# Mixture of experts on Trainium2: a pair's down product ahead of the next pair's second up product

## The chip, the cores and the metric

The kernel runs on one core of one Trainium2 chip. A core has TensorE for matrix products, VectorE, ScalarE and GpSimd for everything elementwise, SyncE for issuing transfers, and 16 transfer engines that all queues share. The metric is the device time of one execution in microseconds. The median of several runs counts. Beside it one execution was profiled; its rows are quoted below.

## The reference

Two transformer-like blocks follow each other, over 512 tokens of width 1024, in float32. The change concerns the second half of the first block, a mixture of 32 experts of which each token takes two:

```python
e_w, e_idx = lax.top_k(jax.nn.softmax(e_logits, axis=-1), TOP_K)      # TOP_K = 2
weight = g_gate * e_w
...
hid = jax.nn.silu(jnp.einsum('td,edf->tef', tk, w1)) * jnp.einsum('td,edf->tef', tk, w3)
hid = hid * c[:, :, None].astype(hid.dtype)
return jnp.einsum('tef,efd->td', hid, w2)
```

w1 and w3 are 1024x256 for each expert and w2 is 256x1024: 1.048 MB each, 100.7 MB over all experts. The rest (a spatial gate and an attention with differences ahead of the experts; a delta rule and a stick-breaking attention behind them) is untouched by the change.

## The kernel before, in words

The program is written by hand: `tensor`, `vector`, `scalar`, `gpsimd` and `sync` each issue one engine's instructions, in the order in which they stand, and wait on each other by semaphores. An engine never passes a wait. What stands behind it in the program waits too.

**Pairs.** The experts are taken two at a time, 16 pairs (expert n and n + 16). Each expert has 64 places for tokens, so a pair fills the 128 partitions. For pair m:

- GpSimd's `gather` (the transfer at L2737) fetches the pair's token rows from `xn_scratch` in HBM by the table `slot_tokens` into one of two buffers `XG`. 1024 rows of 4 KB are fetched in all. It waits for `bring(m - 2)` to have read the buffer.
- TensorE's `bring` (L826; its transposes are at L526, eight of 128x128) turns the rows. ScalarE's and VectorE's `half_tokens` copy a half each to `TOK`.
- TensorE's `up(m, 0)` (L836, matmuls at L848) is the product with w1. ScalarE's `gate_half` takes its sigmoid and VectorE's `gated` multiplies (L1708).
- `up(m, 1)` is the product with w3. VectorE multiplies it in, with the token's weight, in the second part of `gated` (L1713).
- `hand_over` (L854, two transposes at L526, called the hidden turns below) turns the hidden layer and ScalarE's `hidden` copies it to `HT`.
- `down` (L863, matmuls at L876) is the product with w2, in two halves. ScalarE's and VectorE's `half_rows` (VectorE's is L1721) copy a half each to `YO`.
- GpSimd's `add_rows` (the scatter, L2748) adds the rows of `YO` to `x2_scratch` in HBM, one scatter at a time.

The transposes of `bring` are called the token turns below. Most of ScalarE's work has the line of a helper, L2134.

**TensorE's order before** is

```python
bring(0)
for m in range(PAIRS):
    up(m, 0)
    if m:
        hand_over(m - 1)
    else:
        bring(1)
    up(m, 1)
    if m:
        down(m - 1)
        if m + 1 < PAIRS:
            bring(m + 1)
```

and GpSimd's is gather 0, gather 1, then for each m: gather(m + 2), scatter(m). So gather(m + 2) stands behind scatter(m - 1).

**Weights.** SyncE's `load` (L2808) brings the 96 weight matrices of the experts as units of 1.048 MB, six for a pair, in the order of the list `units` that `pair_up` and `pair_down` fill. They land in 19 buffers in turn (`landing_order`: parts of `y_plain`, `raw`, `w_plain`, `h_plain`, `merged` and `scratch`), and TensorE reads them there. A load into a buffer waits until the product that read the unit before is done. `unit` tells a product where its units begin.

Behind the experts, SyncE reads `x2_scratch` back (L2869) when the last scatter has landed, and the second block begins with a norm.

Of the kernel before, what the change touches and what calls it, by code (L numbers as in the profile page):

```python
# [109 lines left out]
def build(nc, x, norm1_g, w_in, v_norm_g, w_s, b_s, q_norm_g, k_norm_g, lambda_q1, lambda_k1,  # L110
# [9 lines left out]
    KD = D // P  # L120
# [12 lines left out]
    PAIRS = NE // 2  # L133
# [154 lines left out]
    units, unit = [], {}  # L288
# [7 lines left out]
    def pair_of(m):  # L296
        return m, m + PAIRS

    def pair_up(m):
        unit["up", m] = len(units), 4  # L300
        for w in (w1, w3):
            for n in pair_of(m):
                units.append([(lambda a: a.rearrange("p (k f) -> p k f", k=KD),
                               w[0, n].rearrange("(p k) f -> p k f", k=KD))])

    def pair_down(m):
        unit["down", m] = len(units), 2
        for n in pair_of(m):
            units.append([(lambda a: a.rearrange("p (k n) -> p k n", k=2),
                           w2[0, n].rearrange("(p k) n -> p k n", k=2))])  # L310
# [22 lines left out]
    MOE = len(units)  # L333
    for m in range(PAIRS + 1):
        if m < PAIRS:
            pair_up(m)
        if m:
            pair_down(m - 1)
    TWO = len(units)
    for b in range(3):  # L340
        matrix(("qa", b), W_IN2, D, BANK * b)
# [68 lines left out]
    def inside(*key):  # L410

        return PS[:, bank.of[key] if not pe.counting else 0, :]
# [102 lines left out]
    def tensor(e):  # L515
# [132 lines left out]
        for b in range(2):  # L648
            product("va", b, False, hthi, htlo, by_k=lambda k: ve["out", "n1", k])
            if b == 0:  # L650
                on.wait_ge(*po["spatial"])
                for half in range(2):
                    ps = fresh("wst", half)
                    for g in range(4):
                        m = turn(ps[:, g * P:g * P + P], wsn[:, half * 4 + g, :])
# [9 lines left out]
            for g in range(4):  # L665
# [4 lines left out]
                for i in range(NT):  # L670
                    m = e.matmul(ps[:, i * P:i * P + P], vn_a[:, i, g * P:g * P + P], wst[:, gg, :], start=True,
                                 stop=True)
# [134 lines left out]
        for j in range(NT):  # L807
            m = e.matmul(rp[:, j + 1:, :], ones, both[:, j, :].unsqueeze(1).broadcast_to([P, NT - j, NE]), start=False,
                         stop=j == NT - 1, skip_group_check=True)
# [4 lines left out]
        for n in range(2 * NT):  # L814
            m = e.matmul(ps[:, 0:COLS], is_place[:, n, :], val[:, 0, n, :], start=n == 0, stop=n == 2 * NT - 1)
# [4 lines left out]
        for n in range(2 * NT):  # L820
            m = e.matmul(ps[:, 0:COLS], is_place[:, n, :], val[:, 1, n, :], start=n == 0, stop=n == 2 * NT - 1)
# [4 lines left out]
        def bring(m):  # L826

            on.wait_ge(*xg_got[m % 2][m])
            for a in range(2):
                ps = fresh("bring", m, a)  # L830
                for k in range(HB):
                    t = turn(ps[:, k * P:k * P + P], XG[:, m % 2, a * HB + k::KD])
                t.then_inc(*pe.mark("bring", m, a))
                bank.filled(("bring", m, a))

        def up(m, a):  # L836

            u, j = m % 2, unit["up", m][0] + 2 * a
            ps = fresh("up", m, a)
            w = [raw_place(j + x).rearrange("p (k f) -> p k f", k=KD) for x in range(2)]  # L840
            on.wait_ge(*ac["out", "bring", m, 0])
            on.wait_ge(*ve["out", "bring", m, 1])
            for x in range(2):
                on.wait_ge(*raw_got[raw_slot[j + x]][j + x])
            for k in range(KD):
                for x in range(2):
                    rows_ = slice(x * CAP, x * CAP + CAP)
                    t = e.matmul(ps[rows_, 0:DE], TOK[:, u, k, rows_], w[x][:, k, :], start=k == 0, stop=k == KD - 1)  # L848
            t.then_inc(*pe.mark("up", m, a))
            for x in range(2):  # L850
                pe.also("unit", j + x)
            bank.filled(("up", m, a))
# [30 lines left out]
        for m in range(PAIRS):  # L883
            up(m, 0)
            if m:
                hand_over(m - 1)
            else:
                bring(1)
            up(m, 1)
            if m:  # L890
                down(m - 1)
                if m + 1 < PAIRS:
                    bring(m + 1)
        hand_over(PAIRS - 1)
        down(PAIRS - 1)

# [3 lines left out]
        with e.If(v):  # L900
# [4 lines left out]
            for j in range(EXTRA):  # L905
                more.wait_ge(*ov_xg[j])
                for k in range(KD):
                    m = e.transpose(OVT[:, k // HB, k % HB * P:k % HB * P + P], oxg[:, k::KD], ident)
# [3 lines left out]
                for k in range(KD):  # L912
                    m = e.matmul(OVU, ogt[:, k, :], w13[:, :, k, :], start=k == 0, stop=k == KD - 1)
                m.then_inc(*ov_pe.mark("up", j))
                more.wait_ge(*ov_ve["gated", j])
                for k in range(2):
                    m = e.transpose(OVT[:, 0, k * P:k * P + P], osg[:, k::2], ident)
                m.then_inc(*ov_pe.mark("hidden", j))
                more.wait_ge(*ov_ve["hidden", j])
                for half in range(2):  # L920
                    cols = slice(half * BANK, half * BANK + BANK)
                    for k in range(2):
                        m = e.matmul(OVD[:, half, :], oht[:, k, :], wdn[:, k, cols], start=k == 0, stop=k == 1)
# [25 lines left out]
        for k in range(KD):  # L949
            m = passes(ps[0:NB, :], wbah[:, k, :], wbal[:, k, :], hthi[:, k, :], htlo[:, k, :], k == 0, k == KD - 1)  # L950
# [293 lines left out]
    def vector(e):  # L1244
# [453 lines left out]
        def half_tokens(m):  # L1698
            on.wait_ge(*pe["bring", m, 1])
            if m > 1:  # L1700
                on.wait_ge(*pe["up", m - 2, 1])
            e.tensor_copy(TOK[:, m % 2, HB:, :], inside("bring", m, 1).rearrange("p (k n) -> p k n", k=HB)).then_inc(
                *ve.mark("out", "bring", m, 1))

        def gated(m):
            u = m % 2
            on.wait_ge(*ac["sigmoid", m])
            tt(SG[:, u, :], SG[:, u, :], inside("up", m, 0)[:, 0:DE], MUL).then_inc(*ve.mark("out", "up", m, 0))  # L1708
            on.wait_ge(*pe["up", m, 1])
            if m > 1:  # L1710
                on.wait_ge(*pe["hidden", m - 2])
            settle()
            stt(HID[:, u, :], SG[:, u, :], info[:, m:m + 1], inside("up", m, 1)[:, 0:DE], MUL, MUL).then_inc(  # L1713
                *ve.mark("out", "up", m, 1))
            ve.also("hid", m)
# [5 lines left out]
            e.tensor_copy(YO[:, m % 2, BANK:], inside("down", m, 1)).then_inc(*ve.mark("out", "down", m, 1))  # L1721

        half_tokens(0)
        half_tokens(1)
        for m in range(PAIRS):
            gated(m)
            if m:
                half_rows(m - 1)
                if m + 1 < PAIRS:
                    half_tokens(m + 1)  # L1730
        half_rows(PAIRS - 1)
        split()
        ve.also("experts")
# [381 lines left out]
    def scalar(e):  # L2115
# [287 lines left out]
        def half_tokens(m):  # L2403
            on.wait_ge(*pe["bring", m, 0])
            if m > 1:
                on.wait_ge(*pe["up", m - 2, 1])
            act(TOK[:, m % 2, 0:HB, :], inside("bring", m, 0).rearrange("p (k n) -> p k n", k=HB), ACT.Copy).then_inc(
                *ac.mark("out", "bring", m, 0))
# [7 lines left out]
        def hidden(m):  # L2416
            on.wait_ge(*pe["hidden", m])
            if m > 1:
                on.wait_ge(*pe["down", m - 2, 1])
            act(HT[:, m % 2], inside("hidden", m)[:, 0:2 * P].rearrange("p (k n) -> p k n", k=2), ACT.Copy).then_inc(  # L2420
                *ac.mark("out", "hidden", m))
# [8 lines left out]
        for m in range(PAIRS):  # L2430
            gate_half(m)
            if m:
                hidden(m - 1)
            else:
                half_tokens(1)
            if m:
                half_rows(m - 1)
                if m + 1 < PAIRS:
                    half_tokens(m + 1)
        hidden(PAIRS - 1)  # L2440
        half_rows(PAIRS - 1)
        split()
# [494 lines left out]
```

## Time and profile before

| | |
|---|---|
| median of 3 runs | 1462.85 us (1461.64 to 1464.62) |
| the profiled execution, its own time | 1465.2 us |
| its span, first to last instruction | 1463.4 us |
| TensorE matmuls busy | 1327.1 us, 91% |
| TensorE granted clock, mean share | 0.962 |
| VectorE, ScalarE, GpSimd busy | 46%, 34%, 4% |
| HBM read | 196.33 MB |
| 16 transfer engines, weights' and other loads' queue | 34.6% |

Busy times are shares of the whole span, which has stages with different limits; the expert stage lies at about 600 to 850 us. The granted clock is a share of 2.4 GHz: 1.0 is that, 0.50 is 1.2 GHz, and values between are mixtures within the stretch. "DMA share" is the mean busy share of the 16 transfer engines (rounding takes it to 1.02 when they are full). In an instruction's row the names are those of the program's buffers, output first, and the bracket at its end has the idle time ahead of it and what ended that. float32 products and transposes appear in the profile twice as often as in the program.

### The profile page before, as it was taken

Reading aid. Unit: us, or ns where it says so; the run is one execution under the profiler, and the core shown is the slowest. Engines: PE = TensorE matmul, PEld = TensorE weight load, DVE = VectorE, ACT = ScalarE, POOL = GpSimd, SP = SyncE. Lnnn points to the kernel's source line nnn. Section 1 sums busy time; section 2 is a strip of 40 time slices with the busy share of each in tenths; the row PEclk is TensorE's granted clock in tenths of the full one; section 3 lists DMA queues with packets and bytes.
Section 4 is the critical chain, followed back from the end, with each engine's and each line's share of the span. In section 5 each row is a group of like instructions: output and inputs, shape, how many; then the busy total and the mean of one; then the engine's idle time right before and its main releaser. Section 6 shows DMA issues by size and latency. Waiting matters only on the chain.

```text
span 1463.4 us, 16683 instructions
## 1 busy us (share of the span) xinstructions
PE 1327.1 (91%) x7019; PEld 1019.3 (70%) x7019; DVE 677.3 (46%) x1045; ACT 494.9 (34%) x768; POOL 53.6 (4%) x59
## 2 busy tenths in 40 slices
PE   6999999999998996788887839999989989899998
PEld 5888887668766885555544428777968876578887
DVE  4454335765577446211111148747566454413253
ACT  4333234446345423011111144444232235422231
POOL 0000000000000000011211100000000000000000
PEclk9999999999999997699999969999999999899999
DMA  6222322112222368899999942102010020112331
GB/s 220 85 87 87 115 73 75 55 58 87 87 86 87 119 239 326 338 401 402 408 402 409 348 133 86 58 1 72 16 51 9 29 87 1 58 58 86 106 124 58
DMA packets 67268, 205.85 MB, mean 141 GB/s; under 512 B 9091, under 2 KB 10229, under 8 KB 54902
## 3 DMA queue, kind: packets, MB, share of 16 engines
q1 hardware_dynamic: 60658, 190.02, 34.6%
q0 software_dynamic: 5824, 12.60, 3.0%
q10 hardware_dynamic: 708, 2.13, 0.4%
q8 instruction: 57, 0.93, 0.3%
q14 instruction: 21, 0.17, 0.0%
HBM read 196.33 MB, written 16.78 MB: 146 GB/s over the span
## 4 chain that ended last, share of the span: by engine, by line
PE 71%; DVE 11%; DMA 10%; ACT 5%; issue 3%; POOL 0%; SPq 0%; DVEq 0%; POOLq 0%; ACTq 0%
PE PS L529 16%; PE PS L531 16%; PE PS L530 16%; PE PS L994 5%; PE PS L526 4%; DMA work<-xn_scratch,slot_tokens 4%; PE PS L848 3%; DMA raw<-in_w 2%; DMA scratch<-in_w 2%; PE PS L876 2%; PE PS L1172 2%; DVE wlo L1263 2%; DVE smalls L1255 1%; ACT work L2134 1%; PE PS L714 1%
## 5 line engine op out<-in xcount | busy, mean ns | idle before, releaser
L1263 DVE TENSOR_TENSOR wlo<-raw,whi 128x2048 fp32r<-128x2048 f32 x72 | 164.9, 2290 | 280.9 <-ACT whi L2134 280.7
L2134 ACT ACTIVATE whi<-raw 128x2048 fp32r<-128x2048 f32 x72 | 137.6, 1911 | 236.3 <-PE PS L531 219.9
L529 PE MATMUL PS<-whi,hthi 128*128 128x512 f32 x480 | 196.0, 408 | 5.7 <-ACT y_plain L2134 4.1
L529 PE MATMUL PS<-hthi,whi 128*128 128x512 f32 x480 | 197.9, 412 | 0.8 <-DVE htlo L1296 0.8
L2134 ACT ACTIVATE work<-PS 128x512 f32<-128x512 f32 (+3 forms) x150 | 82.6, 563 | 316.2 <-PE PS L876 91.3
L531 PE MATMUL PS<-hthi,wlo 128*128 128x512 f32 x480 | 188.7, 393 | 0.0
L530 PE MATMUL PS<-htlo,whi 128*128 128x512 f32 x480 | 188.4, 392 | 0.0
L531 PE MATMUL PS<-whi,htlo 128*128 128x512 f32 x480 | 188.2, 392 | 0.0
L530 PE MATMUL PS<-wlo,hthi 128*128 128x512 f32 x480 | 188.1, 392 | 0.0
L529 PEld LDWEIGHTS PS<-hthi,whi 128*128 128x128 f32 x480 | 91.0, 190 | 32.7 <-issue 14.2
L526 PE MATMUL PS<-consts,work 128*128 128x128 f32 x456 | 71.5, 303 | 43.2 <-DVE work L1290 24.4
L529 PEld LDWEIGHTS PS<-whi,hthi 128*128 128x128 f32 x480 | 91.0, 190 | 24.2 <-ACT y_plain L2134 4.3
L526 PEld LDWEIGHTS PS<-consts,work 128*128 128x128 f32 x456 | 60.4, 172 | 67.2 <-DVE work L1290 25.5
L531 PEld LDWEIGHTS PS<-hthi,wlo 128*128 128x128 f32 x480 | 91.0, 190 | 19.8
L531 PEld LDWEIGHTS PS<-whi,htlo 128*128 128x128 f32 x480 | 90.7, 189 | 19.5
L530 PEld LDWEIGHTS PS<-htlo,whi 128*128 128x128 f32 x480 | 91.3, 190 | 15.8 <-issue 0.2
L530 PEld LDWEIGHTS PS<-wlo,hthi 128*128 128x128 f32 x480 | 91.0, 190 | 16.0 <-issue 0.2
L2134 ACT ACTIVATE scratch<-PS 128x512 f32<-128x512 f32 (+3 forms) x80 | 41.9, 533 | 112.0 <-PE PS L526 57.1
L529 PE MATMUL PS<-yhi,whi 128*128 128x512 f32 x192 | 75.7, 394 | 0.3 <-DVE wlo L1263 0.3
L531 PE MATMUL PS<-yhi,wlo 128*128 128x512 f32 x192 | 74.8, 390 | 0.0
L530 PE MATMUL PS<-ylo,whi 128*128 128x512 f32 x192 | 74.8, 389 | 0.0
L1255 DVE TENSOR_REDUCE smalls<-scratch 128x2 f32<-128x256 f32 (+5 forms) x37 | 37.7, 1018 | 27.9 <-ACT scratch L2134 26.8
(335 smaller groups left out, 1829.6 us busy)
## 6 DMA issues: line engine op xcount, KB each, us to landing
raw<-in_w_in SPq DMA_DIRECT2D x44, 1024.0 KB, 5.0
y_plain<-in_w SPq DMA_DIRECT2D x21, 1024.0 KB, 26.1
w_plain<-in_w SPq DMA_DIRECT2D x20, 1024.0 KB, 22.3
h_plain<-in_w SPq DMA_DIRECT2D x20, 1024.0 KB, 25.6
raw<-in_w SPq DMA_DIRECT2D x15, 1024.0 KB, 20.4
merged<-in_w SPq DMA_DIRECT2D x10, 1024.0 KB, 28.0
scratch<-in_w SPq DMA_DIRECT2D x10, 1024.0 KB, 29.9
raw<-in_w_gate SPq DMA_DIRECT2D x8, 1024.0 KB, 5.1
```

The lines of the kernel that those rows point to most:

```text
L526: return e.transpose(o, i, ident[0:n, 0:n])
L529: e.matmul(o, lh, rh, start=start, stop=False)
L530: e.matmul(o, lh, rl, start=False, stop=False)
L531: return e.matmul(o, ll, rh, start=False, stop=stop)
L714: m = e.matmul(ps[:, i * P:i * P + P], AT[:, n % 2, k * P:k * P + P], vN[:, k, h * P:h * P + P], start=k == 0, stop=k == i)
L848: t = e.matmul(ps[rows_, 0:DE], TOK[:, u, k, rows_], w[x][:, k, :], start=k == 0, stop=k == KD - 1)
L876: t = e.matmul(ps[rows_, :], HT[:, u, k, rows_], w[x][:, k, cols], start=k == 0, stop=k == 1)
L994: m = e.matmul(ps[:, h, :], l[:, h, :], r[:, h, :], start=True, stop=True)
L1172: m = e.matmul(z[:, u, o + (j2 - j) * P:o + widths[j]], tri if j2 == j else nones, SP_[:, pair % 2, u, offs[j2]:offs[j2] + widths[j2]], st ...
L1255: return e.tensor_reduce(o, a, AX_X, op, negate=neg)
L1263: tt(lo, raw_place(j), as_f32(hi), SUB).then_inc(*ve.mark("lo", j))
L2134: return e.activation(o, i, f, bias=bias, scale=scale)
```

## The change

It has three parts.

- **Order of the products.** TensorE's loop becomes up(m, 0), hidden turns of m - 1, token turns of m + 1, down(m - 1), up(m, 1). Before it was up(m, 0), hidden turns, up(m, 1), down(m - 1), token turns.
- **Orders of the others to match.** VectorE's `gated` is cut in two (`gated` and `hidden`) with the token copy and the down copy between them; ScalarE's token copy goes ahead of its down copy.
- **Units.** The first two up units of a pair, the two down units of the pair before, the second two up units: the order of use. `unit["up", m, a]` now has two entries of two units.

GpSimd's program and the number and sizes of all transfers stay.

```diff
--- before.py
+++ after.py
@@ -296,12 +296,11 @@
     def pair_of(m):
         return m, m + PAIRS
 
-    def pair_up(m):
-        unit["up", m] = len(units), 4
-        for w in (w1, w3):
-            for n in pair_of(m):
-                units.append([(lambda a: a.rearrange("p (k f) -> p k f", k=KD),
-                               w[0, n].rearrange("(p k) f -> p k f", k=KD))])
+    def pair_up(m, a):
+        unit["up", m, a] = len(units), 2
+        for n in pair_of(m):
+            units.append([(lambda a: a.rearrange("p (k f) -> p k f", k=KD),
+                           (w1, w3)[a][0, n].rearrange("(p k) f -> p k f", k=KD))])
 
     def pair_down(m):
         unit["down", m] = len(units), 2
@@ -333,9 +332,11 @@
     MOE = len(units)
     for m in range(PAIRS + 1):
         if m < PAIRS:
-            pair_up(m)
+            pair_up(m, 0)
         if m:
             pair_down(m - 1)
+        if m < PAIRS:
+            pair_up(m, 1)
     TWO = len(units)
     for b in range(3):
         matrix(("qa", b), W_IN2, D, BANK * b)
@@ -835,7 +836,7 @@
 
         def up(m, a):
 
-            u, j = m % 2, unit["up", m][0] + 2 * a
+            u, j = m % 2, unit["up", m, a][0]
             ps = fresh("up", m, a)
             w = [raw_place(j + x).rearrange("p (k f) -> p k f", k=KD) for x in range(2)]
             on.wait_ge(*ac["out", "bring", m, 0])
@@ -884,13 +885,11 @@
             up(m, 0)
             if m:
                 hand_over(m - 1)
-            else:
-                bring(1)
-            up(m, 1)
+            if m + 1 < PAIRS:
+                bring(m + 1)
             if m:
                 down(m - 1)
-                if m + 1 < PAIRS:
-                    bring(m + 1)
+            up(m, 1)
         hand_over(PAIRS - 1)
         down(PAIRS - 1)
 
@@ -1706,6 +1705,9 @@
             u = m % 2
             on.wait_ge(*ac["sigmoid", m])
             tt(SG[:, u, :], SG[:, u, :], inside("up", m, 0)[:, 0:DE], MUL).then_inc(*ve.mark("out", "up", m, 0))
+
+        def hidden(m):
+            u = m % 2
             on.wait_ge(*pe["up", m, 1])
             if m > 1:
                 on.wait_ge(*pe["hidden", m - 2])
@@ -1721,13 +1723,13 @@
             e.tensor_copy(YO[:, m % 2, BANK:], inside("down", m, 1)).then_inc(*ve.mark("out", "down", m, 1))
 
         half_tokens(0)
-        half_tokens(1)
         for m in range(PAIRS):
             gated(m)
+            if m + 1 < PAIRS:
+                half_tokens(m + 1)
             if m:
                 half_rows(m - 1)
-                if m + 1 < PAIRS:
-                    half_tokens(m + 1)
+            hidden(m)
         half_rows(PAIRS - 1)
         split()
         ve.also("experts")
@@ -2431,12 +2433,10 @@
             gate_half(m)
             if m:
                 hidden(m - 1)
-            else:
-                half_tokens(1)
+            if m + 1 < PAIRS:
+                half_tokens(m + 1)
             if m:
                 half_rows(m - 1)
-                if m + 1 < PAIRS:
-                    half_tokens(m + 1)
         hidden(PAIRS - 1)
         half_rows(PAIRS - 1)
         split()
```

TensorE in the middle of the expert stage, before. L848 is an up product, L876 a down product, L526 x2 the hidden turns and x8 the token turns.

```order
L848 MATMUL PS<-raw,work 64x256 x16
L876 MATMUL PS<-w_plain,work 64x512 x8
L526 MATMUL PS<-consts,work 128x128 x8
L848 MATMUL PS<-w_plain,work 64x256 x16
L526 MATMUL PS<-consts,work 128x128 x2
L848 MATMUL PS<-h_plain,work 64x256 x16
L876 MATMUL PS<-h_plain,work 64x512 x8
L526 MATMUL PS<-consts,work 128x128 x8
```

The same place with the change (lines are one higher: L849, L877, L527).

```order
L527 MATMUL PS<-consts,work 128x128 x10
L877 MATMUL PS<-raw,work 64x512 x8
L849 MATMUL PS<-w_plain,work 64x256 x32
L527 MATMUL PS<-consts,work 128x128 x10
L877 MATMUL PS<-h_plain,work 64x512 x8
L849 MATMUL PS<-h_plain,work 64x256 x16
```

The token turns have moved up to the hidden turns (x10) and stand ahead of the down product instead of behind it; a pair's second and the next pair's first up product now follow each other (x32).

VectorE in the first pairs of the loop, before. L1702 is the token copy, L1708 and L1713 are the two parts of `gated`, L1721 is the down copy.

```order
L1702 COPY work<-PS 128x512 x2
L1708 TENSOR_TENSOR work<-work,PS 128x256
L1713 SCALAR_TENSOR_TENSOR work<-work,smalls,PS 128x256
L1708 TENSOR_TENSOR work<-work,PS 128x256
L1713 SCALAR_TENSOR_TENSOR work<-work,smalls,PS 128x256
L1721 COPY work<-PS 128x512
L1702 COPY work<-PS 128x512
```

VectorE with the change (token copy L1701, `gated` L1707, `hidden` L1715, down copy L1723).

```order
L1701 COPY work<-PS 128x512
L1707 TENSOR_TENSOR work<-work,PS 128x256
L1701 COPY work<-PS 128x512
L1715 SCALAR_TENSOR_TENSOR work<-work,smalls,PS 128x256
L1707 TENSOR_TENSOR work<-work,PS 128x256
L1701 COPY work<-PS 128x512
L1723 COPY work<-PS 128x512
L1715 SCALAR_TENSOR_TENSOR work<-work,smalls,PS 128x256
```

The token copy and the down copy have changed places, and both stand between the two parts of the gate.

## Rows read from the trace of the kernel before

**Rows 1.** Page, part 2: transfer engines' busy tenths in 40 slices.

```profile
DMA  6222322112222368899999942102010020112331
```

**Rows 2.** Stretches of the expert stage; the first row names the columns.

```profile
core 0: us, PE busy (x) PEld busy (x) DVE busy (x) ACT busy (x) POOL busy (x), PEclk, DMA share, GB/s
...
712.00:728.00 16.00, 14.31 (x107) 9.03 (x109) 2.98 (x5) 2.56 (x5) 3.66 (x3) 1.00 1.02 407
...
808.00:824.00 16.00, 11.25 (x66) 5.99 (x64) 2.28 (x4) 1.96 (x4) 0.36 (x1) 0.89 1.00 394
```

**Rows 3.** Waits, 600 to 850 us: total, times, longest.

```profile
PE PS L526 <- DMA work<-xn_scratch,slot_tokens: 15.7, 8, 5.3
```

**Rows 4.** Timeline, one pair: start, length, instruction, idle before with its releaser.

```profile
706.61 3.60 PE L876 MATMUL PS<-w_plain,work 128*64 128x512 f32 x16
...
710.33 0.69 DVE L1721 COPY work<-PS 128x512 f32<-128x512 f32 x1 [3.02 <-PE PS L876]
...
711.87 1.58 POOL L2748 DMA_INDIRECT x_scratch<-work,slot_tokens  x1 [10.21 <-DVE work L1721]
...
712.02 1.16 PE L526 MATMUL PS<-consts,work 128*128 128x128 f32 x8 [1.81 <-DMA work<-xn_scratch,slot_tokens]
...
713.75 1.02 POOL L2737 DMA_INDIRECT work<-xn_scratch,slot_tokens  x1 [0.31 <-issue]
...
714.01 3.67 PE L848 MATMUL PS<-w_plain,work 128*64 128x256 f32 x32 [0.83 <-ACT work L2134]
...
725.09 0.97 PEld L526 LDWEIGHTS PS<-consts,work 128*128 128x128 f32 x8 [0.81 <-DMA work<-xn_scratch,slot_tokens]
```

**Rows 5.** Timeline: two more scatters and the token turns behind them.

```profile
626.58 1.62 POOL L2748 DMA_INDIRECT x_scratch<-work,slot_tokens  x1 [22.89 <-ACT work L2134]
...
640.49 1.16 PE L526 MATMUL PS<-consts,work 128*128 128x128 f32 x8 [2.44 <-DMA work<-xn_scratch,slot_tokens]
...
684.96 1.58 POOL L2748 DMA_INDIRECT x_scratch<-work,slot_tokens  x1 [12.02 <-ACT work L2134]
...
697.08 1.16 PE L526 MATMUL PS<-consts,work 128*128 128x128 f32 x8 [0.35 <-DMA work<-xn_scratch,slot_tokens]
```

**Rows 6.** Gathers and scatters by their index tile.

```profile
DMA to landing us min/median/max: 3.3/10.1/11.9
```

**Rows 7.** Three waits of TensorE and the granted clock (PEclk) behind them.

```profile
1084.65 1.11 PE L526 MATMUL PS<-consts,y_plain 128*128 128x128 f32 x4 [5.55 <-DVE y_plain L1887]
...
1245.71 2.57 PE L1172 MATMUL PS<-scratch,consts 128*128 128x128 f32 x12 [3.14 <-DVE scratch L2036]
...
642.50:647.80 5.30, 5.30 (x33) 3.67 (x33) 0.00 (x0) 0.00 (x0) 0.06 (x1) 0.68 1.03 366
1084.70:1090.00 5.30, 5.30 (x25) 5.30 (x26) 3.89 (x6) 1.98 (x4) 0.00 (x0) 0.50 0.00 0
1245.80:1250.40 4.60, 4.60 (x18) 2.66 (x18) 1.68 (x2) 2.50 (x3) 0.00 (x0) 0.63 0.70 228
```

**Rows 8.** Timeline: hidden turns of pair 0.

```profile
617.43 0.50 PE L526 MATMUL PS<-consts,work 128*128 128x128 f32 x2
```

**Rows 9.** Timeline: end of the expert stage.

```profile
831.68 0.48 DVE L1713 SCALAR_TENSOR_TENSOR work<-work,smalls,PS 128x256 f32<-128x256 f32 x1 [3.21 <-PE PS L848]
...
832.92 0.61 PE L876 MATMUL PS<-merged,work 128*64 128x512 f32 x1 [1.29 <-DMA scratch<-in_w]
...
836.50 0.51 PE L526 MATMUL PS<-consts,work 128*128 128x128 f32 x2
...
837.93 0.61 PE L876 MATMUL PS<-scratch,work 128*64 128x512 f32 x1 [0.93 <-DMA y_plain<-in_w]
...
838.22 1.55 POOL L2748 DMA_INDIRECT x_scratch<-work,slot_tokens  x1 [13.00 <-ACT work L2134]
...
841.70 0.69 DVE L1721 COPY work<-PS 128x512 f32<-128x512 f32 x1 [4.33 <-PE PS L876]
...
847.43 2.52 POOL L2748 DMA_INDIRECT x_scratch<-work,slot_tokens  x1 [7.67 <-DMA x_scratch<-work,slot_tokens]
```

## Prediction

> **What bounds the kernel now.** I read four views in this order: the slices of the span, the stretches of the expert stage, the waits inside it, and then one pair's instructions in order of time. The slices show where the transfers are the full resource: the transfer engines are at 9 tenths only in the middle of the span, which is the expert stage [rows 1]. In a stretch of it the transfer share is 1.02 at 407 GB/s, while TensorE works 14.31 of 16 us; near the end of the stage TensorE falls to 11.25 of 16 with the transfers still full [rows 2]. So the weights set the pace. A pair brings six units of 1.048 MB, 6.29 MB, and its token rows go through twice; 1024 rows of 4 KB each way over 16 pairs are 0.26 MB a way. 6.81 MB at 407 GB/s are **16.7 us a pair**. TensorE runs ahead of that out of the nineteen buffers filled early, and is caught by it at the end.
>
> Second bound, close behind: the tokens. TensorE's matmuls wait for the gather longer than for anything else in the stage, 15.7 us in 8 waits [rows 3]. One pair shows the chain [rows 4]: the down product starts at 706.61 and takes 3.60; VectorE copies its second half at 710.33; GpSimd starts the scatter at 711.87, which is 1.66 us after the product's end, and only behind it, at 713.75, the gather of two pairs later; the token turns that need this gather start at 725.09, having waited for it. Scatter to token turns is 13.2 us. Elsewhere it is 13.9 and 12.1 (626.58 to 640.49, 684.96 to 697.08) [rows 5]. The cause in the trace is the full weight queue: between issue and landing these transfers take 3.3 us at the least, 10.1 in the median, and the least is at an edge of the stage, where few weights are under way [rows 6].
>
> **The change, part by part.** Let E be the end of a pair's down product. GpSimd's order is not touched: the gather for pair m+2 stands behind the scatter of pair m-1. So tokens of m+2 are there no sooner than E(m-1) + 1.66 + 13.2 = E(m-1) + 14.9.
>
> *Before*, TensorE has between E(m-1) and the turns of m+2: turns of m+1, up product, hidden turns, up product, down(m). By rows [rows 4], 725.09 less 710.21 less the 1.8 waited in between is 13.1 us. That nearly covers 14.9, and since the down product of m comes ahead of the wait, a wait is shared by two pairs: 13.1 and 14.9 alternate, 14.0 on average, under the 16.7 of the weights.
>
> *After*, down(m) stands behind the turns of m+2, and the turns of m+2 stand one product earlier. Between E(m-1) and them are left second up(m) 3.6, first up(m+1) 3.6, hidden turns 0.5: 7.7 us. TensorE waits 14.9 - 7.7 = **7.2 us in every pair**, and down(m) waits with it. The next scatter, and with it the next gather, wait for down(m). The loop closes on itself: 1.66 + 13.2 + turns 1.1 + down 3.6 = 19.6 us a pair.
>
> A wait of 7.2 us has a second price. After a wait of 5.55 us TensorE's granted clock is at the lower level (1.2 GHz, share 0.50) for the 5.3 us behind it; after 3.14 it is 0.63 over 4.6; after the 2.44 at 640.49 it is 0.68 over the 5.3 us of the up product, which takes 3.67 otherwise [rows 4, 5, 7]. What is lost is the time by one less the share: 2.7, 1.7, 1.7 us. The work behind the wait is turns and down product, which lie on the loop. I take 2.2, the middle of 1.7 and 2.7. No row has a wait of 7.2 us in each pair, so the bounds are 0 (the clock stays) and 2.7. The Trainium skill, "TensorE: Matmul & The Clock Gate", HAM oscillation, has the same case: a wait for data on each tile makes each next tile start at the low clock; the trace agrees for the waits of 2.44 us and more. By that rule the loop pays every time; if every wait went like the 1.81 at 712.02, after which the up product still took 3.67, it would pay nothing, and the sum would be 13 x 2.2, 29 us, less.
>
> So a pair takes 19.6 + 2.2 = **21.8 us** (weights need 16.7). Transfers then have 5 us of slack, but not where the gather needs it: two units are freed at E, two at E + 3.6, two at E + 7.2, so the weights run from just behind E for 16.7 us without a gap, and scatter and gather lie at E + 1.7 to E + 14.9, inside. That is why I keep 13.2 and do not take 3.3. Bounds for it: 12.1 and 13.9, the ends among the waits of rows 5; far below, 3.3 plus the 1.9 between scatter and gather [rows 4, 6].
>
> The other edits:
> - The token turns no longer stand directly ahead of the up product that needs their copies: 0.83 us a pair less [rows 4]. Nothing, because it lies in time that weights or gather set.
> - The hidden turns get the token turns (1.1 us) behind them instead of an up product, which still covers ScalarE's 0.38 us copy; only in the last pair, without token turns, it costs 0.5 or so, counted below.
> - VectorE and ScalarE: the token copies stand ahead of the down copies, and wait with TensorE for the gather. Queued behind are the down copies and VectorE's second half of the hidden layer, which need products later on TensorE anyway: nothing. Splitting that VectorE function adds no arithmetic.
> - SyncE's queue: 96 loads as before, in the new order of use, so none is asked for before its buffer's turn; same bytes: nothing. Wrong order would show as waits for weights at second up products.
> - Start: pair 0 is unchanged but for the turns of pair 1 on VectorE; the stage's first weights come as before.
>
> **The sum.** The first up product of pair 1 ends before the hidden turns at 617.43 [rows 8]. Then 0.5 + 1.16 + 3.6: down(0) ends at 622.7. Tokens of pair 3 at 622.7 + 14.9 = 637.6, E(1) = 637.6 + 1.1 + 3.6 + 2.2 = 644.5. Twelve loops of 21.8 give E(13) = 906.1. Behind it no gather is left: up, up, down, up, down 5 x 3.6, twice 1.0 for hidden turns and their copy (836.50 to 837.43, [rows 9]), 0.9 for VectorE's hidden layer (831.68, 0.48 long, with the way there and back): 20.9, so the last down product ends at 927.0. Before it ends at about 841.6 (837.93 and 16 matmuls; VectorE's copy starts at 841.70) [rows 9]. That is **+85.4**.
>
> One gain at the end: the last scatter now waits 7.67 us for the one before it, which began at 838.22, and starts at 847.43, though its rows were ready at 841.70 + 0.69 + 0.85 = 843.2 [rows 9]. With down(14) ahead of the last up product, the scatter of 14 starts 7.4 us before the last product's end and its 9.2 us are over about when the last is ready. **-4.0**. Sum: +81.4 on the profiled 1465.2 us (span 1463.4), 1546.6; the median of the runs, 1462.85, is 2.35 lower: **1544.2 us**.
>
> **Rivals.**
> 1. *The gather gets quick and the weights stay the bound.* If scatter to turns falls to 16.7 - 1.66 - 4.7 = 10.3 us or less, the loop is no longer than the weights' pace. Then the last up weights still land by 832.9 [rows 9], up, wait, turns, down give 842.0, 0.4 later than now, and the scatter gains 4.0: 1459.3 us, faster. For it: 3.3 us seen with few weights queued, and the queue gets shorter. Against: all three that are shown took 12.1 us or more beside weights, and the weights run through the window. The Trainium skill, "DMA: Bandwidth & Descriptors", Anatomy of one DMA, prices such a DMA at about 2 us plus bytes by 436 GB/s, 2.6 us for 0.26 MB; by that rule this rival is what happens. The trace disagrees (median 10.1). Chance 0.07.
> 2. *The clock does not fall.* Loop 19.6: E(1) 642.3, E(13) 877.5, end 898.4, +56.8 - 4.0: 1515.6 us. The same time comes out with the clock loss and scatter to turns of 11 us. Chance 0.15, with all of 1495 to 1523.
> 3. *Half and half:* weights and gather both leave room to each other, loop 17 to 19 us: 1463 to 1495. Chance 0.06.
> 4. *The order on the chip is not what I read*, so nothing or only the tail changes: 1459 to 1463. The order rows show the turns ahead of the down product, so 0.02.
>
> My forecast, 1523 to 1560, has 0.70. Its ends: 12.1 and a clock loss of 1.7 give a loop of 20.1, +64 - 4, 1523; 13.9 and 2.7 a loop of 23.0, +101 - 4, 1560. The range for 8 in 10 goes down into rival 2: **1505 to 1560**. A difference under 0.2% (3 us) cannot be told from none here. Slower by more: 0.92; within: 0.03; faster: 0.05, which is rival 1 where all of its gain comes.
>
> **What would show it.** In the profile after: token turns wait for the gather in 13 pairs, over 90 us in all instead of 15.7; pairs follow each other at 21.8 us; transfer share in the stage about 0.75; granted clock in it 0.8 or so; no waits for weights; last scatter without a wait of over 1 us. A loop at 16.7 with share 1.02 shows rival 1; waits as long as I say but clock at 1.0 shows rival 2. I am wrong at the root if token turns wait less than 3 us a pair.

## The result

The changed kernel takes **1543.12 us** (median of 4 runs, 1539.66 to 1546.11), the one before 1463.73 us in the same comparison. The ratio is 1.0542, 95% interval 1.0514 to 1.0570: 79 us slower. The forecast was 1544.2 us, 1505 to 1560.

The profiled execution took 1539.66 us, 3.5 us under the median, with a span of 1537.9 us against 1463.4. In its waits from 600 to 930 us (columns as in [rows 3]) the gather now leads by far among TensorE's matmuls, and no line for TensorE names a weight buffer:

```profile
PE PS L527 <- DMA work<-xn_scratch,slot_tokens: 99.8, 13, 8.7
```

It was 15.7 us in 8 waits [rows 3]. Stretches of the expert stage, columns as in [rows 2]:

```profile
706.00:728.00 22.00, 14.45 (x96) 7.87 (x94) 2.29 (x4) 2.05 (x5) 2.60 (x2) 0.84 0.81 308
...
728.00:750.00 22.00, 14.01 (x88) 7.63 (x86) 2.28 (x4) 1.56 (x4) 2.61 (x2) 0.77 0.82 311
...
750.00:772.00 22.00, 14.05 (x94) 7.73 (x92) 2.29 (x4) 2.03 (x5) 2.61 (x2) 0.84 0.81 309
...
882.00:904.00 22.00, 17.42 (x112) 9.00 (x110) 2.98 (x5) 2.56 (x5) 2.60 (x2) 0.90 0.53 168
```

The first three answer to 712 to 728 in [rows 2]. The transfers are no longer full (0.81 and 0.82 instead of 1.02), TensorE works 14.0 to 14.5 of 22 us instead of 14.31 of 16, and the clock, 1.00 there before, is at 0.77 to 0.84. The last stretch lies at the end, where few weights are left. One pair in the timeline, which answers to [rows 4]:

```profile
751.79 0.69 DVE L1723 COPY work<-PS 128x512 f32<-128x512 f32 x1 [4.97 <-PE PS L877]
...
753.32 1.58 POOL L2748 DMA_INDIRECT x_scratch<-work,slot_tokens  x1 [19.61 <-DVE work L1723]
...
755.21 1.03 POOL L2737 DMA_INDIRECT work<-xn_scratch,slot_tokens  x1 [0.31 <-issue]
...
758.50 0.51 PE L527 MATMUL PS<-consts,work 128*128 128x128 f32 x2
...
766.96 1.97 PE L527 MATMUL PS<-consts,work 128*128 128x128 f32 x8 [7.95 <-DMA work<-xn_scratch,slot_tokens]
...
768.86 4.47 PE L877 MATMUL PS<-h_plain,work 128*64 128x512 f32 x16
...
773.46 0.69 DVE L1723 COPY work<-PS 128x512 f32<-128x512 f32 x1 [3.79 <-PE PS L877]
...
774.99 1.58 POOL L2748 DMA_INDIRECT x_scratch<-work,slot_tokens  x1 [18.76 <-DVE work L1723]
```

The scatter starts 1.66 us after its down product's end (at 751.66), the gather 1.89 behind it, the token turns (L527 x8) 13.64 us behind the scatter after a wait of 7.95 us; turns and down product run partly at the lower clock (1.97 instead of 1.16 us, 4.47 instead of 3.60), and the next scatter starts 21.7 us after the last. The page's slices show the stage longer, and the transfer engines at 7 and 8 tenths in most of it instead of 9, against [rows 1]:

```profile
DMA  6222321113214388977877743210100012103231
```

The end of the stage, which answers to [rows 9]:

```profile
914.64 0.69 DVE L1723 COPY work<-PS 128x512 f32<-128x512 f32 x1 [3.79 <-PE PS L877]
...
916.18 1.55 POOL L2748 DMA_INDIRECT x_scratch<-work,slot_tokens  x1 [9.89 <-DVE work L1723]
...
923.32 0.69 DVE L1723 COPY work<-PS 128x512 f32<-128x512 f32 x1 [4.81 <-PE PS L877]
...
924.82 2.92 POOL L2748 DMA_INDIRECT x_scratch<-work,slot_tokens  x1 [7.08 <-DVE work L1723]
```

The last down product ends at 923.2 (841.6 before). The last scatter waits for VectorE's copy alone, 1.6 us after the product, and no more for the scatter ahead of it (5.8 us before).

One correction to the section on the profile before: a float32 product appears in the profile twice as often as in the program, a transpose once.

### The profile page after: what moved, and what is told of

Same layout as the page of the kernel before. It is cut to its first block, busy times and chain, and to the rows that moved or that the text cites. A ratio compares the mean times of both kernels' runs of the same rounds, so it can differ in the third digit from the quotient of the medians.

```text
span 1537.9 us, 16683 instructions
## 1 busy us (share of the span) xinstructions
PE 1337.4 (87%) x7019; PEld 1016.9 (66%) x7019; DVE 677.0 (44%) x1045; ACT 494.9 (32%) x768; POOL 54.1 (4%) x59
## 4 chain that ended last, share of the span: by engine, by line
PE 68%; DMA 11%; DVE 11%; ACT 4%; issue 3%; POOL 1%; SPq 0%; POOLq 0%; DVEq 0%; ACTq 0%
PE PS L530 15%; PE PS L532 15%; PE PS L531 15%; DMA work<-xn_scratch,slot_tokens 10%; PE PS L527 5%; PE PS L877 5%; PE PS L993 4%; DVE wlo L1262 2%; PE PS L1171 2%; POOL x_scratch L2748 1%; DVE smalls L1254 1%; ACT work L2136 1%; ACT whi L2136 1%; PE PS L715 1%; ACT scratch L2136 1%
## 5 line engine op out<-in xcount | busy, mean ns | idle before, releaser
L527 PE MATMUL PS<-consts,work 128*128 128x128 f32 x456 | 81.4, 333 | 128.6 <-DMA work<-xn_scratch,slot_tokens 105.0
L527 PEld LDWEIGHTS PS<-consts,work 128*128 128x128 f32 x456 | 67.8, 177 | 143.0 <-DMA work<-xn_scratch,slot_tokens 107.6
L530 PEld LDWEIGHTS PS<-hthi,whi 128*128 128x128 f32 x480 | 90.8, 189 | 32.7 <-issue 14.5
L532 PEld LDWEIGHTS PS<-hthi,wlo 128*128 128x128 f32 x480 | 90.4, 188 | 19.6
L1701 DVE COPY work<-PS 128x512 f32<-128x512 f32 x16 | 11.1, 691 | 125.8 <-PE PS L527 125.8
## 6 DMA issues: line engine op xcount, KB each, us to landing
h_plain<-in_w SPq DMA_DIRECT2D x20, 1024.0 KB, 10.2
```

The costliest lines, as they stand in the source:

```text
L527: return e.transpose(o, i, ident[0:n, 0:n])
L530: e.matmul(o, lh, rh, start=start, stop=False)
L532: return e.matmul(o, ll, rh, start=False, stop=stop)
```

## The experiments

Ratios are against the kernel before, timed on the same chip in the same rounds.

| run | what differs | median us | ratio (95%) |
|---|---|---|---|
| e1 | change, gather ahead of scatter | 1459.9 | 0.9978 (0.9967 to 0.9990) |
| e5 | before, token turns alone moved | 1543.8 | 1.0545 (1.0524 to 1.0566) |
| e4 | change, token turns put back behind down | 1460.2 | 0.9978 (0.9968 to 0.9987) |
| e2 | before, gather ahead of scatter | 1462.8 | 0.9995 (0.9985 to 1.0005) |
| e6 | change, 7 filler matmuls in the wait | 1525.6 | 1.0435 (1.0407 to 1.0463) |
| e8 | change, 8 filler matmuls | 1516.0 | 1.0362 (1.0347 to 1.0378) |
| e7 | change, a quarter of the weights' bytes | 1444.8 | 0.9889 (0.9863 to 0.9915) |
| e3 | e1 with units in the old order | 1465.1 | 1.0014 (1.0003 to 1.0025) |
| e9 | change with units in the old order | 1524.4 | 1.0405 (1.0383 to 1.0428) |
| e10 | e1 and e4 together | 1457.7 | 0.9969 (0.9956 to 0.9982) |

### Is it the loop over scatter and gather?

e1 opens the loop on GpSimd and touches nothing else of the change:

```diff
-        for m in range(2):
+        for m in range(3):
             gather(m)
         for m in range(PAIRS):
-            if m + 2 < PAIRS:
-                gather(m + 2)
+            if m + 3 < PAIRS:
+                gather(m + 3)
             add_rows(m)
```

> The changed kernel with one edit on GpSimd: the gather for pair m+3 ahead of the scatter of pair m, instead of the gather for m+2 (so a gather no longer stands behind the scatter whose rows TensorE has just made). My theory, the loop over scatter and gather: the loop is open, no token turns wait over 1 us, a pair goes at the weights' 16.7 us, transfer share in the stage 1.02, median 1459 us (1456 to 1464). Rival, the order of the products or of the weights' units is itself at fault: 1535 us or more, with waits elsewhere.

Measured 1459.9 us: the whole loss is gone, and 3 us of gain are left. Its waits from 600 us on name one wait for a gather, at the stage's start:

```profile
PE PS L527 <- DMA work<-xn_scratch,slot_tokens: 5.3, 1, 5.3
```

Its stretch from 640 to 800 us is at the weights' bound again, share 1.02 at 405 GB/s:

```profile
640.00:800.00 160.00, 130.16 (x936) 78.15 (x934) 24.64 (x43) 21.57 (x44) 26.35 (x21) 0.98 1.02 405
```

Gathers and scatters are hardly quicker here (10.0 us in the median from issue to landing, 10.5 in the change). The gathers are asked for a pair earlier. So the loss was the loop, not the order of products as such. The expectation that no turns wait over 1 us held but for this first wait, which lies ahead of the loop.

e2 makes the same edit in the kernel before.

> The kernel before with the same GpSimd edit as the first run. Theory: before is bound by the weights, its 15.7 us of waits for the gather lie beside them, so nothing is won: 1462 us, within 0.2% of before, transfer share 1.02 as before. Rival, that these waits were on the path: 1450 us or less.

1462.8 us, ratio 0.9995 (0.9985 to 1.0005): no change that can be measured, though in its trace TensorE waits for no gather behind the stage's first. In the kernel before that first wait is 5.3 of the 15.7 us; the other seven, 10.4 us in all, cost nothing: with them gone, the weights still set the time.

### Which part of the change closes it?

e5 takes the kernel before and moves the token turns alone; VectorE and ScalarE follow. The diff shows TensorE's loop from the second up product on (the turns of pair 1, too, now stand behind it).

```diff
             up(m, 1)
+            if m + 1 < PAIRS:
+                bring(m + 1)
             if m:
                 down(m - 1)
-                if m + 1 < PAIRS:
-                    bring(m + 1)
```

> The kernel before with one thing of the change alone: the token turns of m+1 stand ahead of the down product of m-1, which itself stays behind the second up product; units in the order of before. Theory: the down product, and so the next gather, waits for the token turns; the loop is 1.66 + 13.6 + 1.2 + 3.6 + 2.2 for the clock, about 22 us, median 1544 us (1530 to 1555). Rival, that it takes the earlier down product too (less TensorE work between scatter and turns): near 1463 us.

e4 keeps the down product where the change puts it and puts the turns back behind it:

```diff
-            if m + 1 < PAIRS:
-                bring(m + 1)
             if m:
                 down(m - 1)
+            if m + 1 < PAIRS:
+                bring(m + 1)
             up(m, 1)
```

> The changed kernel with the token turns put back behind the down product, both still ahead of the second up product. Theory: between the end of down(m-1) and the turns of m+2 stand two up products, hidden turns, down(m) and again none of it waits for that gather; two pairs take 14.9 + 12.9 = 27.8 us, 13.9 a pair, under the weights' 16.7, so median 1460 us (1457 to 1465) and waits for the gather under 30 us in all. Rival, that less lead for the gather is what costs (11.8 us of work instead of 13.1 before): a wait of 3 us in every pair, transfers no longer full, 1480 us or more.

e5 has the whole loss (1543.8 us), e4 has none (1460.2). The waits of e5:

```profile
PE PS L526 <- DMA work<-xn_scratch,slot_tokens: 96.0, 13, 8.6
```

And those of e4:

```profile
PE PS L527 <- DMA work<-xn_scratch,slot_tokens: 17.6, 11, 6.0
```

The down product's move costs nothing by itself, although it shortens the work between a scatter and the turns that need the gather behind it. The exchange of token turns and down product is what lets every wait delay the next gather: in e5 the scatter is 13.4 us ahead of the turns in the mean of the first twelve loops, near the change's 13.6, and waits and loss are the change's.

### What is the clock's share?

e6 fills the wait with work that nobody reads (seven matmuls of 128x512 float32 ahead of the token turns of pairs 3 to 15):

```diff
+            if m > 1 and m + 1 < PAIRS:
+                ps = fresh("filler", m)
+                for _ in range(7):
+                    e.matmul(ps, ident, C[:, 0:BANK], start=True, stop=True)
+                bank.filled(("filler", m))
             if m + 1 < PAIRS:
                 bring(m + 1)
```

> The changed kernel with seven matmuls of 128x512 (some 6 us of work whose result nobody reads) ahead of each pair's token turns from pair 2 on, in the time in which TensorE would wait. Theory: they delay nothing, but keep the granted clock up, so that turns and down product take 4.8 instead of about 7 us: 12 loops less 2.2 each, median 1516 us (1510 to 1524), granted clock in the stage near 1.0. Rival, the clock costs nothing on this path because something else bounds the loop: 1540 us or more.

1525.6 us, 17.6 less than the change, but 10 more than the theory's number. The timeline of one pair in e6:

```profile
688.90 6.17 PE L891 MATMUL PS<-consts 128*128 128x512 f32 x14
...
696.93 1.18 PE L527 MATMUL PS<-consts,work 128*128 128x128 f32 x8 [1.86 <-DMA work<-xn_scratch,slot_tokens]
...
698.04 5.29 PE L877 MATMUL PS<-h_plain,work 128*64 128x512 f32 x16
```

Two stretches of the same pair:

```profile
690.00:697.00 7.00, 5.14 (x13) 1.97 (x11) 0.00 (x0) 0.00 (x0) 0.00 (x0) 1.00 1.02 409
...
697.00:700.00 3.00, 3.00 (x14) 1.63 (x16) 0.69 (x1) 0.60 (x1) 0.00 (x0) 0.66 0.99 421
```

The fillers take 6.2 us and leave a wait of 1.86, and behind that the clock still falls (0.66 from 697 to 700; down product 5.29 us). That happens in three of the twelve pairs in which a wait is left: turns and down product take 6.1 to 6.4 us in them and 4.7 in the others. The length of the wait that is left does not sort them: it fell behind 1.86, 2.01 and 2.47 us, and not behind 2.81. Three such pairs are some 5 us; the rest of the 10 has no single cause in these rows. e8 has eight fillers:

> As the run with seven idle matmuls ahead of the token turns, but eight. With seven, a wait of 1.9 us was left in the pairs and the clock still fell in some of them (0.66 behind 696.93, down product 5.29 instead of 3.60). Theory: with one us left it falls in none, a pair takes 1.66 + 13.5 + 1.1 + 3.6 = 19.9 us, median 1516 us (1512 to 1520). Rival, the fillers delay the turns themselves: no gain over the 1525.6 of seven, or a loss of 9 us.

1516.0 us, the number expected. The granted clock from 640 to 860 us is 0.99, against 0.81 in the change, and the waits for the gather are 12.5 us in all instead of 99.8. In one pair the clock fell all the same, behind a wait of 1.86 us (6.4 us for turns and down product). The stretch in e8:

```profile
640.00:860.00 220.00, 208.78 (x1160) 107.64 (x1158) 24.57 (x44) 21.58 (x44) 28.72 (x22) 0.99 0.88 338
```

The same stretch in the change:

```profile
640.00:860.00 220.00, 140.78 (x894) 77.16 (x892) 22.85 (x40) 19.00 (x39) 26.08 (x20) 0.81 0.81 310
```

27.1 us over 13 pairs are 2.1 us each. The traces agree: turns and down product of the first twelve loops take 4.9 us in the mean instead of 6.9, with scatter to turns unchanged (13.6 us in both). In the thirteenth pair, whose gather is quick, the fillers outlast the wait and hold the turns up by some 2 us (an estimate from its gather's landing). Adding idle work makes this kernel 27 us faster. It shows that the clock was on the path and that the fillers lay, in the twelve loops, in time that was lost anyway.

### Why does the gather take that long?

e7 cuts the transfers of all weight units of the experts behind the first 19: an up unit brings one of its eight slices, a down unit one of two. The products run as often as before on what lies in the buffers, so this kernel leaves most of the weights out of its result; it is there for its times alone.

```diff
             for place, src in units[j]:
+                if j >= MOE + len(slots) and j < TWO:
+                    e.dma_start(place(raw_place(j))[:, 0:1, :], src[:, 0:1, :]).then_inc(*raw_got[raw_slot[j]].mark(j))
+                    continue
                 e.dma_start(place(raw_place(j)), src).then_inc(*raw_got[raw_slot[j]].mark(j))
```

> The changed kernel with all but the first 19 weight units of the experts cut short: an up unit brings an eighth of its bytes, a down unit a half, a quarter of a pair's bytes in all, so the rest of the weights are left out of the computation. Theory: gathers are slow because they share the transfer engines with the weights, so scatter to turns falls from 13.6 to 6 to 9 us, the wait of 7 us falls to nearly nothing, a pair takes 13 to 15 us: median 1425 to 1450 us. Rival, the 13.6 us are GpSimd's own or fixed costs of such transfers: still 1535 to 1545 us.

1444.8 us. Time from issue to landing of gathers and scatters in e7, by their index tile:

```profile
DMA to landing us min/median/max: 3.4/5.5/7.4
```

In the change:

```profile
DMA to landing us min/median/max: 3.3/10.5/12.5
```

The median falls from 10.5 to 5.5 us, with the same number and size of gathers and scatters. About half of the time is the company of the weights. In e7 the clock also stays up behind most of the waits that are left (1.1 to 2.1 us) and falls behind the last two (3.3 us and more), so its time is no price of the transfers alone. The change itself has a natural case: in the last loop, whose window has few weights, there are 10.3 us from scatter (886.43) to turns (896.70) instead of 13.6.

### And the order of the weights' units?

e3 is e1 with the list of units as before (four up units, then two down units):

```diff
         if m < PAIRS:
             pair_up(m, 0)
+            pair_up(m, 1)
         if m:
             pair_down(m - 1)
-        if m < PAIRS:
-            pair_up(m, 1)
```

> As the first run (gather ahead of the scatter, changed order of the products), but with the weights' units in the order of before, all four up units of a pair ahead of the down units of the pair before. Theory: TensorE is ahead of the weights in most of the stage, where order within eight units does not matter, and at the end down(14) waits for its units while the up units lie there: within 3 us of the first run. Rival, the order of the units carries weight: over 8 us slower than the first run.

1465.1 us, 5.2 more than e1: more than I had expected. The end of e3 in the timeline:

```profile
833.29 1.08 PE L876 MATMUL PS<-merged,work 128*64 128x512 f32 x1 [5.36 <-DMA scratch<-in_w]
...
839.15 0.69 DVE L1722 COPY work<-PS 128x512 f32<-128x512 f32 x1 [10.78 <-PE PS L876]
...
849.32 2.91 POOL L2747 DMA_INDIRECT x_scratch<-work,slot_tokens  x1 [7.11 <-DVE work L1722]
```

The same of e1:

```profile
832.33 0.40 PE L849 MATMUL PS<-merged,work 128*64 128x256 f32 x1 [1.34 <-DMA scratch<-in_w]
...
841.32 0.69 DVE L1723 COPY work<-PS 128x512 f32<-128x512 f32 x1 [4.80 <-PE PS L877]
...
842.82 1.54 POOL L2748 DMA_INDIRECT x_scratch<-work,slot_tokens  x1 [8.68 <-DVE work L1723]
```

In e3 the second last down product waits 5.36 us for its units, which there come behind the up units; at 833.29 it, the last up product and the last down product are still to do, while in e1 at 832.33 only the last two are. The last scatter starts 6.5 us later. So where weights are the bound, the order of units is worth 5 us at the end of the stage.

e9 is the change itself with the old order of units:

> The changed kernel with the weights' units in the order of before and nothing else put back. Theory: with the loop at 22 us a pair the transfers have slack, so the units' order costs and gains nothing: 1543 us, within 3. Rival, the units carry part of the loss as they did at the end of the run without the loop (5 us): 1548 us or more, with waits for weights at down products.

1524.4 us, **18.8 us less** than the change. Both of my expectations were wrong. SyncE's loads (SPq) and GpSimd around one scatter in e9:

```profile
768.78 1.58 POOL L2747 DMA_INDIRECT x_scratch<-work,slot_tokens  x1 [17.89 <-DVE work L1722]
...
770.62 1.96 SPq L2807 DMA_DIRECT2D h_plain<-in_w  x4
...
770.66 1.03 POOL L2736 DMA_INDIRECT work<-xn_scratch,slot_tokens  x1 [0.30 <-issue]
...
779.73 1.97 PE L526 MATMUL PS<-consts,work 128*128 128x128 f32 x8 [5.27 <-DMA work<-xn_scratch,slot_tokens]
```

The same in the change:

```profile
773.38 4.28 SPq L2808 DMA_DIRECT2D h_plain<-in_w  x4
...
774.99 1.58 POOL L2748 DMA_INDIRECT x_scratch<-work,slot_tokens  x1 [18.76 <-DVE work L1723]
...
776.88 1.02 POOL L2737 DMA_INDIRECT work<-xn_scratch,slot_tokens  x1 [0.30 <-issue]
...
788.51 1.76 PE L527 MATMUL PS<-consts,work 128*128 128x128 f32 x7 [7.83 <-DMA work<-xn_scratch,slot_tokens]
```

In the change the down product's two buffers are the next in SyncE's order, so their loads start as soon as it ends, 1.6 us ahead of the scatter. In e9 the order names the second up product's buffers first; SyncE waits for those, and the weights start again 1.8 us behind the scatter (1.5 to 1.9 in each of the twelve loops). The scatter gets through before the weights are in full flow (it lands after 5.6 us instead of 10.2, in the median of the first thirteen), and the gather behind it lands after 10.1 instead of 11.5: 10.9 us from scatter to turns in this pair, 11.8 in the mean of the twelve between 623 and 864 us, against 13.6 in the change. 12 times 1.8 is 22 us; turns and down product take 0.3 us more a pair there (7.2 instead of 6.9), which leaves 18. The two kernels were timed in different comparisons; by their ratios, 1.0542 and 1.0405, the difference is 20.0 us.

e5 is a check on this. Its list of units is e9's, the order of before, but there the down product again stands where the list has it, and the weights start ahead of the scatter once more:

```profile
757.60 4.28 SPq L2807 DMA_DIRECT2D w_plain<-in_w  x4
...
759.21 1.58 POOL L2747 DMA_INDIRECT x_scratch<-work,slot_tokens  x1 [19.54 <-DVE work L1722]
```

Its scatter to turns is 13.4 us and it has the change's 1543.8 us. So the list of units matters through the start of the weights that it gives with the order of use. That the later start is the cause is read from these rows and agrees with e7; no run moved the start alone.

### Both openings together

> Both orders that opened the loop in one kernel: gather for m+3 ahead of the scatter of m, down product ahead of the second up product, token turns behind the down product. Theory: each alone is at the weights' bound and has the gain of the last scatter, so both together give no more: 1459 to 1461 us. Rival, the waits for the gather left with the turns behind (17.6 us) still cost something: 1456 us or less.

1457.7 us, ratio 0.9969 (0.9956 to 0.9982), 5 us faster than the kernel before and the fastest version here. It lies between theory and rival, and its interval overlaps with those of e1 and e4; whether the two edits add up stays open.

## Why the prediction was right, and where it was not

**The loop.** Right, and its terms too. Token turns from 634.03 to 877.21 are eleven loops of 22.1 us (forecast 21.8): 1.66, scatter to turns 13.6 in the mean of the first twelve (forecast 13.2, bounds 12.1 and 13.9; the longest was 14.4), and 6.9 for turns and down product, which is the 1.1 + 3.6 + 2.2 of the forecast. 13 waits, 99.8 us in all, were forecast as 13 and over 90; the transfer share, forecast at about 0.75, was 0.81. e1 shows the loop, e5 and e4 show that the turns' place ahead of the down product closes it.

**The clock.** 2.2 forecast. Turns and down product take 4.7 us where the clock stays up (e8) and 6.9 in the mean of the change: 2.2, between 1.3 and 2.9, a small and a large loss in turn; the medians of e8 and the change give 2.1. Rival 2 priced a clock that stays up at 1515.6 us; held up by fillers, it gave 1516.0. So close a match is luck too: in e8 the first down product ends 3.5 us sooner than priced and a loop is 20.1 us instead of 19.6. The Trainium skill, "TensorE: Matmul & The Clock Gate", HAM oscillation, describes a clock that falls at each wait for data. The trace agrees: behind each of the change's 13 waits the turns took 1.97 instead of 1.16 us, and the granted clock was 0.81 from 640 to 860 us.

**Rival 1** failed on its first condition: scatter to turns stayed at 13.2 us or more in the twelve loops beside the weights, and was 10.3 only in the last. Its mechanism is real, as e7 shows. Its price, and rival 3's, do not come out of the forecast's own sum. A loop of 16.7 us from 622.7 on ends the last product at 622.7 + 13 x 16.7 + 20.9 = 860.7, 19.1 us later than before, and gives 1478 us, not 1459.3; loops of 17 and 19 give 1482 and 1508, not 1463 to 1495. The kernel before is through at 841.6 because from its down(0) on a pair takes 14.4 us in the mean, out of buffers filled early, so 15.3 us a loop and 8.9 from scatter to turns would have been the condition. The forecast itself did not use these prices. The Trainium skill, "DMA: Bandwidth & Descriptors", Anatomy of one DMA, has about 2 us plus the bytes for such a transfer. The traces do not agree: beside weights they show 10.5 us in the median, with a quarter of them 5.5, and 3.3 at the least.

**SyncE's queue at nothing.** This step failed. I wrote that loads in order of use cost and gain nothing because none is asked for before its turn. I had placed the weights' start "just behind E" myself and did not see that the order of units is what puts it there. e9 measures it at 18.8 of the change's 79 us. It cannot be added to a loop that e1 removes whole: it is a part of the loop's length. The sum held all the same because the 13.2 us were read beside weights that were under way at the scatter (in the kernel before, too, loads go out 1.6 us ahead of the scatters at 626.58, 684.96 and 711.87), as they are in the change. With the loop open the same reorder gains 5.2 us (e3 to e1), which I had also at nothing.

**The end.** -4.0 forecast. The last scatter starts 1.6 instead of 5.8 us after the last product: 4.2. e1 and e4, which have no loop, are 3 us faster than before, near the 3.6 that rival 1 carried over from this term; in their traces the last scatter starts at 842.8 and 843.6 instead of 847.4. No run isolates the term.

**The sum** came out within 1.1 us of the median, and that is partly luck. In the profiled execution the last product ends at 923.2, not 927.0, out of terms of either sign. The stage began earlier and left the low clock sooner (the turns of pair 1 start at 605.3 instead of 609.3), so down(0) ends at 618.5, not 622.7: 4.2 less. The next twelve loops, from one down product's end to the next, took 22.2 instead of 21.8 us: 4.7 more. The thirteenth took 18.3: 3.5 less. What follows took 20.1 instead of 20.9. The part behind the stage took 3 us less than in the profile before. Differences of 3 to 4 us are within the spread of the runs, 1539.66 to 1546.11.

## What to carry to other kernels

When an instruction is moved ahead of another on an in-order engine, follow what the second one releases: a wait that two pairs shared before now came in every pair and delayed the next gather too, since the scatter that the down product feeds stands ahead of the gather that the token turns need. Here, putting the prefetch (the gather) ahead of the write-back (the scatter) in their queue made the order of products free again. Look at an order of loads as well: it decides when the bulk transfers start, and so what a small urgent transfer meets.

## What I had not expected of the hardware

- A wait of 1.86 us can have a lower clock behind it (e6: 0.66 over the 3 us behind 697), while the 1.81 us at 712.02 in [rows 4] was followed by an up product at full length, and 2.81 us in another pair of e6 by turns and down product at full speed. The length of the wait alone did not tell.
- Weights that start 1.8 us behind a scatter instead of 1.6 us ahead of it come with 1.8 us less on the mean way from the scatter to the turns, and 18.8 us less for the kernel, with all bytes the same.
- A long and a short weight queue slow the gather alike: 13.2 us from scatter to turns before, with weight loads that took 20 to 30 us from issue to landing, and 13.6 after, where they took 8 to 12 (medians by buffer).
